# Differential attention on TensorE: the projection bank placed behind the scores in every step

## What is computed

```python
def diff_attend(q, k, v, lam_params, lam_init, subln_w):
    ...
        p1 = jax.nn.softmax(jnp.einsum("bhqd,bhkd->bhqk", q1, k1).astype(jnp.float32) * scale, axis=-1)
        p2 = jax.nn.softmax(jnp.einsum("bhqd,bhkd->bhqk", q2, k2).astype(jnp.float32) * scale, axis=-1)
        a = (p1 - lam * p2).astype(v.dtype)
        return jnp.einsum("bhqk,bhkd->bhqd", a, v)
    ...
    o = rms_norm(o, subln_w) * (1.0 - lam_init)
```

## Time and profile before

| | |
|---|---|
| median of 3 runs | 3893.29 us (3891.92 to 3895.60) |
| the profiled execution's own time | 3895.62 us |
| its span, first to last instruction | 3893.8 us |
| granted TensorE clock over the span, share of full speed | 0.942 |
| PE busy | 3421.9 us, 88% |
| DVE, ACT, POOL busy | 47%, 30%, 25% |
| the heads of the differential attention | about 256 to 970 us of the span |

### The profile page before, as it was taken

How to read it: one execution, slowest core, us unless ns; L and a number is a source line. 1 busy time by engine, 2 the same in 40 slices (tenths; PEclk the granted TensorE clock), 3 DMA queues, 4 the chain that set the end, 5 groups by cost and what they waited for, 6 DMA issues and landing times. The chain is left out here.

```text
span 3893.8 us, 53499 instructions
## 1 busy us (share of the span) xinstructions
PE 3421.9 (88%) x20703; PEld 3143.3 (81%) x20703; DVE 1834.4 (47%) x2407; ACT 1172.8 (30%) x2115; POOL 974.0 (25%) x733
## 2 busy tenths in 40 slices
PE   5479999997899999999855788888689999999997
PEld 1178888886889999999845667677569999999996
DVE  0435555555165455455441444444433555555555
ACT  0234444444131122112221444444342322112211
POOL 0112222222332233223321122222114223223221
PEclk7689999998999999999977999999899999999998
DMA  9521111212211111111023222232231111111101
GB/s 392 227 69 44 43 43 43 51 37 107 87 53 46 38 38 49 38 38 40 30 72 92 49 80 69 73 82 81 73 146 51 48 35 52 38 38 38 54 27 54
DMA packets 209505, 268.94 MB, mean 69 GB/s; under 512 B 31396, under 2 KB 174365, under 8 KB 202077
## 3 DMA queue, kind: packets, MB, share of 16 engines
q1 hardware_dynamic: 201373, 244.23, 20.0%
q0 software_dynamic: 7856, 22.29, 1.6%
q10 hardware_dynamic: 144, 0.52, 0.0%
HBM read 198.57 MB, written 35.91 MB: 60 GB/s over the span
## 5 line engine op out<-in xcount | busy, mean ns | idle before, releaser
L454 PE MATMUL psum<-Hh,wh 128*128 128x384 f32 x3264 | 1109.4, 340 | 106.7 <-POOL wl L1460 38.6
L456 PE MATMUL psum<-Hl,wh 128*128 128x384 f32 x3264 | 1099.3, 337 | 0.0
L455 PE MATMUL psum<-Hh,wl 128*128 128x384 f32 x3264 | 1099.3, 337 | 0.0
L454 PEld LDWEIGHTS psum<-Hh,wh 128*128 128x128 f32 x3264 | 619.2, 190 | 116.0 <-POOL wl L1460 38.8
L535 DVE SCALAR_TENSOR_TENSOR x<-psum,mod,x 128x384 f32<-128x384 f32 (+2 forms) x768 | 377.6, 515 | 684.5 <-PE psum L456 641.5
L455 PEld LDWEIGHTS psum<-Hh,wl 128*128 128x128 f32 x3264 | 619.4, 190 | 0.0
L456 PEld LDWEIGHTS psum<-Hl,wh 128*128 128x128 f32 x3264 | 618.8, 190 | 0.0
L818 POOL TENSOR_TENSOR wl<-wr,wh 128x1024 fp32r<-128x1024 f32 x88 | 219.8, 2497 | 997.8 <-ACT wh L744 997.8
L950 DVE SCALAR_TENSOR_TENSOR ff_c<-ff_u,par,ff_c 128x1153 f32<-128x1153 f32 x176 | 412.2, 2342 | 16.9 <-DVE ff_c L947 5.2
L775 ACT ACTIVATE ff_u<-psum 128x768 f32<-128x768 f32 x88 | 71.6, 813 | 1111.0 <-PE psum L456 1111.0
L454 PE MATMUL psum<-ff_ah,ff_dh 128*128 128x384 f32 x1056 | 364.6, 345 | 28.6 <-POOL ff_al L840 20.7
(11 more groups left out here) (218 smaller groups left out, 4532.1 us busy)
## 6 DMA issues: line engine op xcount, KB each, us to landing
in_mw<-mod_w SPq DMA_DIRECT2D x48, 1024.0 KB, 8.8
wr<-w_up SPq DMA_DIRECT2D x88, 512.0 KB, 3.9
ff_dr<-w_down SPq DMA_DIRECT2D x22, 1024.0 KB, 6.0
wr<-w_qkv_diff SPq DMA_DIRECT2D x24, 512.0 KB, 4.1
ga_ks<-k_save SPq DMA_DIRECT2D x8, 1280.0 KB, 5.5
x<-x_save SPq DMA_DIRECT2D x16, 576.0 KB, 9.1
ga_qsh<-ga_nqh SPq DMA_DIRECT2D x32, 288.0 KB, 4.7
ga_qsl<-ga_nql SPq DMA_DIRECT2D x32, 288.0 KB, 5.4
```

The costliest lines, as they stand in the source:

```text
L454: pe.matmul(out, w_hi, m_hi, start=start, stop=False)
L455: pe.matmul(out, w_lo, m_hi, start=False, stop=False)
L456: return pe.matmul(out, w_hi, m_lo, start=False, stop=stop)
```

## The change

In steps 1 to 8 of a head the projection bank, if there is one, comes first in the list. Before, that was so in step 8 alone (`STEPS - 2`), and in steps 1 to 7 it stood behind the transposes. PE so runs scores, `W`, `T`, then what followed; the banks of 6 and 7 are dealt anew along the changed list; and ACT, which asks whether `W` is first, changes its order in steps 1 to 7 too.

```diff
@@ -1237,7 +1237,7 @@
         if s == STEPS - 1:
             return tiles + [("PV", 4), ("ST", 3), ("ST", 4)] + [("W+",)] * ahead2 + [("BC", 3), ("BC", 4)]
         proj = [("W",) + PROJ[s]] if ahead else []
-        u = proj + tiles if s == STEPS - 2 else tiles + proj
+        u = proj + tiles if True else tiles + proj
         u += [("PV", p) for p in PV_AT.get(s, [])]
         u += [("ST", p) for p in ST_AT.get(s, [])]
         if ahead and s in (2, 3):
```

## The result

| | before | changed kernel |
|---|---|---|
| median of 4 runs each | 3894.44 us | 3921.31 us (3914.06 to 3925.42) |
| ratio, 95% interval | | 1.0067 (1.0049 to 1.0084) |
| the profiled execution's own time | 3895.62 us | 3922.13 us |
| its span | 3893.8 us | 3920.3 us |
| granted clock over the span | 0.942 | 0.942 |

The change makes the kernel 26.9 us slower, where the forecast was 22.9 us and 3916 us, in a range of 3905 to 3928. The profiled executions lie 26.5 us apart.

A forecast was written before the change was run, and what follows sets the result against it. TensorE, busy 88% of the span, was taken to bound the kernel, so only its own sequence matters. P·V's 2.55 us plus statistics' 0.72 make 3.27 us a head, 22.9 over seven heads: 3916 us, range 3905 to 3928.

The forecast's parts named there:

- P·V's steps: Steps 2, 4 and 6, P·V (product with the values) behind the transposes: +0.74 us wait, +0.11 longer P·V, +0.85 each.
- step 8's picture: Step 8 of the old kernel, already in the new order: P·V 2.25 us after the first transpose, 3.99 us long.
- Steps 5 and 7: Statistics (ST) behind the transposes wait for group 1's bank, start at 1.87 us against 1.51: +0.36 us each.
- Step 3: ST, then the new keys' transpose (ko), which gets group 2's bank after 2.25 us, as before: 0.
- Step 1: Next tile's scores behind the transposes use six other banks and wait only for exponentials: 0, at most 0.36 us.
- the one exposed projection of the upper bound: One projection at half clock beside the loop's turn, 4.3 us more, counted in the upper bound.
- What was to stay covered: Scores' wait for exponentials, projection's copy on ACT, combined probabilities and projection weights stay hidden, costing nothing.
- Rival A: ACT becomes late, exponentials end after the projection and copies slip: +24.5 us, 3941 us; chance 0.06.
- Rival B: Clock falls behind transposes and wait, P·V takes 5.6 instead of 3.9 us in 21 steps: +36, 3952 us; chance 0.04.
- the rule of the Trainium skill: A transpose does not count as busy for the clock as a matmul does, so transposes beside a wait are riskier.
- Rival C: Only P·V's waits count, ST's bank is free: 17.9 us, 3911 us; chance 0.07.
- Rival D: Three stalls at the loop's turn and their clock falls vanish, returning 15.4 us: +7.5, 3901 us; chance 0.03.

The follow-up runs named there:

- pv_steps: Kernel before with the new order only in steps 2, 4 and 6, besides step 8: 3914.20 us, ratio 1.0048.
- late_wait: Changed kernel, P·V waiting for the last transpose group's copy only before its seventh key chunk: 3909.33 us, ratio 1.0035 to the kernel before.
- again: The changed kernel measured once more, unchanged: 3921.11 us against 3894.95, ratio 1.0068.
- act_order: Kernel before with only ScalarE's order changed, both exponentials ahead of the transpose copies in steps 1 to 7 of seven heads: 4146.42 us, ratio 1.0656.
- no_exception: Kernel before with the old order (transposes, then projection) in step 8 too: 3907.07 us, ratio 1.0037.
- odd_steps: Kernel before with the new order only in steps 1, 3, 5 and 7, besides step 8: 3900.12 us, ratio 1.0011.

## Why the prediction was right

The mechanism is the forecast one, and each run that took a part of it away or left a part in place moved by about that part. The measured median lies 5 us above 3916: 1.1 us are the other median of the kernel before (3894.4, not 3893.3), 2.9 the terms below that were too small. The last 1 us is within the scatter of the medians; in the profiled executions it is the clock.

- *P·V's steps.* Forecast 0.85, measured 0.87 us in 21 steps. pv_steps has it alone, 18.7 us in the heads; late_wait takes 0.38 us of each back. In step 6 the parts differ a little from step 8's picture, the wait being 0.67 us and P·V 3.96 long, and the step grows by the same 0.87.
- *Steps 5 and 7: the term that was too small.* The wait came out at the forecast 1.87 us, but I added 0.36 where the step grew by 0.49: step 5 takes 4.29 + 1.87 + 0.54 = 6.70 us from projection to scores instead of 6.21. I had given P·V 0.11 us for a start behind a wait, and ST nothing; it has the same 0.11 (0.54 against 0.43, 402.03 to 402.46 in the kernel before). The other 0.02 is the projection in front of transposes, 4.29 against 4.27. I also expected 14 waits of some 0.3 us at ST: there are 21, step 3 included, and the profile shows 0.20 each, since it counts from the end of the last transpose.
- *Step 3.* Forecast 0, measured 0.09 (6.87 against 6.78 us). The reason given for the 0 was not what happened: ko was to wait for group 2's copy, 2.25 us after the first transpose, with ST hidden in that wait. But ko has no wait in the trace. ST starts at 1.87 us, takes 0.47, and ko starts right behind it at 2.34 us (386.13 to 388.47), which is the 0.09.
- *Step 1.* Forecast 0, measured 0 (5.89 us against 5.88).
- *Sum.* 3 × 0.87 + 2 × 0.49 + 0.09 = 3.7 us a head instead of 3.27, 25.8 us for seven. The remaining 0.9 us of the profiled difference are what is left of two things at the loop: head 0 grew by 4.81 us, 0.9 of it in a projection of 5.17 us, since the clock stayed at half for 6.8 us there and not for 3.4 (the stretch below), and head 1 grew by only 3.30 us, since its stall at the loop's turn was 0.38 us shorter. The long projection is the one exposed projection of the upper bound, at 0.9 us and not 4.3; that it came in this execution and not in the second one (again) is chance.

```profile
261.70:268.50 6.80, 5.87 (x27) 0.51 0.07 19
```

- *What was to stay covered, stayed:* scores wait 4 times; ACT had its margin; PE's list of waits has none for the weights.
- *Rival A* didn't come. *Rival B* neither: steps 4 and 5 of head 1 run at a granted clock of 1.00 (the stretch below), from there to the last head the clock was below 1.00 only at the two turns of the loop (456.3 to 459.7 and 647.5 to 654.3 us), and P·V never took more than 3.99 us in the 21 steps. Here the rule of the Trainium skill ("TensorE: Matmul & The Clock Gate", Part 4) did not decide: transposes with two waits of 0.25 and 0.58 us kept the full clock in the changed kernel as in step 8 before. Within the steps of the first seven heads it fell in two other runs, with a wait of 3.6 us (act_order) and, in six of seven cases, with one of 1.66 us (no_exception). Whether transposes beside a wait count for less than matmuls would, these runs don't show, as none put matmuls in their place. The stretch of the changed kernel:

```profile
390.50:410.00 19.50, 18.21 (x112) 1.00 0.12 31
```

- *Rival C* is excluded by ST's waits and odd_steps. *Rival D* didn't come: the stalls at the loop's two turns were 3.12 and 3.35 us instead of 3.50 and 3.39. The third that D counts, on the way into the loop, is a wait for the first copies of v (3.70 us, 3.71 before).

## What to carry to other kernels

When an engine writes and another one empties few buffers, a long piece of independent work belongs behind the producer, in front of the first user of the copies: 4.3 us of projection hide the way of a bank there, and in front of the producer they hide nothing. Look for a place in the old kernel that already has the new order; one step of ten gave nearly all of this forecast's numbers. Where the wait can't be moved, ask which part of the consumer needs the last copy. And where the producer waits for the copy of its own first group, make that group the smallest; it gave 7.8 us in the old order, and nothing in the new one, where the producer waits for the copy of the projection.

## What the runs showed that was not expected

A start behind a wait costs 0.11 us beyond the wait, for P·V and for ST, and the same for waits of 0.20 and 0.58 us; for P·V they lie in its first matmul. What they are made of wasn't shown. And a wait of PE can cost more than itself: 3.6 us of waiting before a projection made the projection 1.2 to 2.4 us longer through the clock, and even one wait of 1.66 us was followed by 3.4 us at half clock in six of seven heads.
